# A twelve-layer network on one core: the first weights of most layers beside the ring, and a convolution's first block in two passes

## The chip, the cores and the metric

The kernel runs on one core of a Trainium2 chip. The metric is the device time of one execution in microseconds, the median of three. TensorE multiplies, VectorE and ScalarE do elementwise work and read PSUM, GpSimd does small roots and issues loads of vectors and tables, and the SyncE queue (SP) issues the loads of the weights.

## What is computed

The reference sends 256 tokens of 1024 channels in float32 through twelve layers, a mixer and a feed-forward network in turn:

```
LAYERS = ("rwkv", "ffn", "moba", "ffn", "conv", "ffn", "near", "ffn", "hyena", "ffn", "conv", "ffn")
first block (layers 0 to 3):   x = layer_norm(ALPHA * x + mixer(x));  x = layer_norm(ALPHA * x + swiglu_ffn(x))
second block (layers 4 to 11): x = x + mixer(rmsnorm(x));             x = x + swiglu(rmsnorm(x))
conv mixer:                    (b_gate * depthwise_conv3(c_gate * u)) @ w_out, with b_gate, c_gate, u = split(h @ w_in)
```

The mixers are a recurrent time mix with a decay (rwkv), two kinds of attention (moba, near), a gated convolution of width 3 (conv) and one by a Fourier transform (hyena). Each has an input projection of 1024 to 3072 channels and an output projection of 1024 to 1024; a feed-forward network goes to 2 x 2816 and back.

## The kernel before

**Weights in quarters.** All large weights come as 588 quarters of 128 x 1024 float32 (512 KB), in the order of their use: 24 + 8 for a mixer, 44 + 22 for an ffn. For each, SP loads `raw` (L333, L339), ScalarE writes a rounded copy `w_hi` (L1169), VectorE writes the rest `w_lo = raw - w_hi` (L1554), and TensorE multiplies in three passes, hi by hi, hi by lo and lo by hi, in the fp32r format. `raw`, `w_hi` and `w_lo` are rings of four slots; quarter q stands in slot q % 4. SP loads a slot anew when its `w_lo` is done (a loop with a wait on `w_lo[s]`); `split` waits for the load and for `w_used`, TensorE's sign that it has used what stood in the slot. `ahead(q, n)` splits the quarters q + 4 and on.

**Blocks.** An input projection goes in blocks of four quarters. `block_tokens` has the tokens as stationary operand, 128 at a time, and moves 512 columns of weights (L361). `block_channels`, for conv and hyena, has 128 columns of weights as stationary operand and moves all 256 tokens (L419). `project` is the output projection (L448), tokens 0 to 127 (t = 0) first in its last four rows, so that the next layer's norm can start on them. `half_done` tells VectorE of each finished half row.

**Boundaries.** `residual` of VectorE adds the projection to the residual X (`add`, L1604 and L1606), forms the moments (layer norm: `add_with_stats`, `moments`, `centred` L1621, `normed` L1628) or waits for the squares of ScalarE (`square`, L1203) and the root of GpSimd (L2374), and writes the normed tokens (`rms_normed`, L1636). TensorE turns them to channels (`turn`, L468), ScalarE takes their rounded copy (`operand`, L1181) and VectorE the rest (`operand`, L1575, which signals `operand_ready`). Among these steps stand the splits of the next layer's first four quarters, whose slots come free only as the last rows of the projection are used. TensorE does t = 0 of the first block, turns t = 1, then does t = 1 (`first_block`); before a conv or hyena layer it waits for both halves and then does all 256 tokens. Matmuls on the identity without use (`keep_busy`, L383) stand in the gaps.

```
            for t in range(TT):
                for i in range(4):
                    if i % 2 == 0:
                        pe.wait_ge(m["operand_ready"], due(m["operand_ready"]))
                    if t == 0:
                        if src is X:
                            keep_busy((0, 0, 3, 1)[i])
                        pe.wait_ge(w_lo[(q + i) % SLOTS], nth(q + i))
                    mm = part_tokens(q, i, 0, t)
```

**Order.** Every engine works its own program in order; semaphores tie them together. The order was written out by hand.

## Time and profile before

| | us |
|---|---|
| median of 3 runs | 2048.99 (2047.09 to 2050.7) |
| the profiled execution, its own time | 2047.56 |
| its span in the profile | 2045.8 |
| TensorE busy | 1986.2 |
| VectorE busy | 1276.6 |
| ScalarE busy | 908.8 |
| GpSimd busy | 161.6 |

Times in the profile are in microseconds from the start of the span, unless marked ns. Busy time counts the `keep_busy` matmuls too. Matmuls are pipelined: the time from the start of one to the start of the next is what one costs, and is shorter than its own duration. The mean granted clock of TensorE is 0.995 of 2.4 GHz.

### The profile page before, as it was taken

What the parts mean: (1) busy time and instruction counts of PE and PEld (TensorE: products, weight loads), DVE (VectorE), ACT (ScalarE), POOL (GpSimd) and SP (SyncE); (2) the same over time, 40 slices, a digit from 0 to 9 for tenths busy, and PEclk for the clock granted to TensorE, in tenths of its full rate; (3) what the DMA queues carried; (4) which work ended last, traced back from release to release, by engine and by line L of the source; (5) the groups of instructions that cost most, each with busy time, mean ns of one, the idle gap of its engine ahead of it and who ended that gap; (6) DMA issues with size and microseconds to landing.
All of it is one profiled execution on the core that took longest, in us unless ns stands there. A gap on an engine that the chain in (4) does not pass through costs nothing.

```text
span 2045.8 us, 32584 instructions
## 1 busy us (share of the span) xinstructions
PE 1986.2 (97%) x12754; PEld 1615.7 (79%) x12754; DVE 1276.6 (62%) x1623; ACT 908.8 (44%) x1282; POOL 161.6 (8%) x198
## 2 busy tenths in 40 slices
PE   7999999999999999999999999999999999999999
PEld 6689688878678879888878678877766888897887
DVE  7774755477665556655667655577886554575554
ACT  4452354434444434444555454434434444434442
POOL 2252100000010010000003011001100000000000
PEclk9999999999999999999999999999999999999999
DMA  8321265555166554565455257553323555555554
GB/s 302 114 63 45 98 216 182 189 170 180 62 201 200 196 185 165 171 210 184 166 190 191 73 167 226 200 185 124 104 83 126 192 185 187 174 167 187 183 171 155
DMA packets 93040, 335.95 MB, mean 164 GB/s; under 512 B 11230, under 2 KB 11364, under 8 KB 92623
## 3 DMA queue, kind: packets, MB, share of 16 engines
q1 hardware_dynamic: 85824, 311.62, 45.9%
q0 software_dynamic: 7120, 22.95, 3.8%
q8 instruction: 72, 1.18, 0.2%
q14 instruction: 24, 0.20, 0.0%
HBM read 332.43 MB, written 1.05 MB: 163 GB/s over the span
## 4 chain that ended last, share of the span: by engine, by line
PE 87%; DVE 8%; issue 2%; POOL 2%; ACT 2%; DMA 0%; SPq 0%; DVEq 0%; ACTq 0%; POOLq 0%
PE acc L361 42%; PE acc L448 20%; PE acc L419 9%; DVE w_lo L1554 2%; PE acc L920 2%; PE aux L841 1%; PE aux L468 1%; PE aux L625 1%; PE aux L876 1%; POOL rstd L2371 1%; PE aux L908 1%; DVE operand_lo L1575 1%; PE aux L897 1%; ACT w_hi L1169 1%; POOL rstd L2374 1%
## 5 line engine op out<-in xcount | busy, mean ns | idle before, releaser
L1554 DVE TENSOR_TENSOR w_lo<-w_raw,w_hi 128x1024 fp32r<-128x1024 f32 x588 | 716.7, 1224 | 569.5 <-ACT w_hi L1169 562.5
L1169 ACT ACTIVATE w_hi<-w_raw 128x1024 fp32r<-128x1024 f32 x588 | 620.6, 1059 | 786.6 <-PE acc L361 456.4
L361 PE MATMUL acc<-w_hi,operand_hi 128*128 128x512 f32 x1344 | 536.7, 399 | 27.0 <-DVE operand_lo L1720 12.1
L361 PE MATMUL acc<-w_hi,operand_lo 128*128 128x512 f32 x1344 | 526.8, 392 | 0.0
L361 PE MATMUL acc<-w_lo,operand_hi 128*128 128x512 f32 x1344 | 526.3, 392 | 0.0
L361 PEld LDWEIGHTS acc<-w_hi,operand_hi 128*128 128x128 f32 x1344 | 253.6, 189 | 91.8 <-DVE operand_lo L1575 15.4
L361 PEld LDWEIGHTS acc<-w_hi,operand_lo 128*128 128x128 f32 x1344 | 253.5, 189 | 54.0
L361 PEld LDWEIGHTS acc<-w_lo,operand_hi 128*128 128x128 f32 x1344 | 254.0, 189 | 50.3 <-issue 0.5
L448 PE MATMUL acc<-w_hi,hidden_hi 128*128 128x512 f32 x528 | 207.9, 394 | 0.0
L448 PE MATMUL acc<-w_hi,hidden_lo 128*128 128x512 f32 x528 | 205.9, 390 | 0.0
L448 PE MATMUL acc<-w_lo,hidden_hi 128*128 128x512 f32 x528 | 205.6, 389 | 0.0
L419 PE MATMUL acc<-operand_hi,w_hi 128*128 128x256 f32 x576 | 171.1, 297 | 0.8 <-DVE operand_lo L1575 0.8
L419 PE MATMUL acc<-operand_hi,w_lo 128*128 128x256 f32 x576 | 164.0, 285 | 0.0
L419 PE MATMUL acc<-operand_lo,w_hi 128*128 128x256 f32 x576 | 164.0, 285 | 0.0
L419 PEld LDWEIGHTS acc<-operand_hi,w_hi 128*128 128x128 f32 x576 | 111.6, 194 | 9.3 <-issue 8.0
L448 PEld LDWEIGHTS acc<-w_hi,hidden_hi 128*128 128x128 f32 x528 | 99.1, 188 | 24.5 <-issue 3.7
L448 PEld LDWEIGHTS acc<-w_hi,hidden_lo 128*128 128x128 f32 x528 | 99.1, 188 | 21.1
L448 PEld LDWEIGHTS acc<-w_lo,hidden_hi 128*128 128x128 f32 x528 | 99.3, 188 | 19.8
L419 PEld LDWEIGHTS acc<-operand_hi,w_lo 128*128 128x128 f32 x576 | 111.5, 194 | 3.6 <-issue 3.6
L419 PEld LDWEIGHTS acc<-operand_lo,w_hi 128*128 128x128 f32 x576 | 111.4, 193 | 0.0
L1181 ACT ACTIVATE operand_hi<-aux 128x512 fp32r<-128x512 f32 x52 | 28.9, 596 | 86.2 <-PE aux L468 85.7
L2383 POOL TENSOR_SCALAR stat<-stat 128x1 f32<-128x1 f32 x16 | 4.8, 303 | 741.1 <-ACT token_scratch L1203 741.0
(474 smaller groups left out, 2111.7 us busy)
## 6 DMA issues: line engine op xcount, KB each, us to landing
w_raw<-in_weights SPq DMA_DIRECT2D x588, 512.0 KB, 3.4
ln_gain<-in_gains POOLq DMA_DIRECT2D x7, 512.0 KB, 5.0
bias_at<-in_rpb POOLq DMA_DIRECT2D x12, 256.0 KB, 5.1
ln_gain<-in_ln_g POOLq DMA_DIRECT2D x4, 512.0 KB, 3.9
ln_bias<-in_ln_b POOLq DMA_DIRECT2D x4, 512.0 KB, 5.1
vec_rw<-in_vec POOLq DMA_DIRECT2D x3, 512.0 KB, 5.6
l_rw<-in_lora SPq DMA_DIRECT2D x1, 1152.0 KB, 10.6
iclr_rw<-in_xT SPq DMA_DIRECT2D x2, 512.0 KB, 4.6
```

The costliest lines, as they stand in the source:

```text
L361: mm = pe.matmul(acc[:, 2 * pair + t, :], (ah, al)[x][:, kt, t * P:(t + 1) * P], W[w][:, s, kk * 512:(kk + 1) * 512], start=(kt == 0 and ( ...
L419: mm = pe.matmul(acc[:, 2 * pair + c // 2, (c % 2) * SEQ:(c % 2 + 1) * SEQ], W[w][:, s, kk * 512 + c * P:kk * 512 + (c + 1) * P], (ah, al) ...
L448: mm = pe.matmul(acc[:, 2 * t + c, :], (hi, lo)[x][:, kt, t * P:(t + 1) * P], W[w][:, s, c * 512:(c + 1) * 512], start=(kt == 0 and (x, w) ...
L468: mm = pe.transpose(aux[:, 2 * t + kt // 4, (kt % 4) * P:(kt % 4 + 1) * P], src[:, t, kt * P:(kt + 1) * P], back(ident[:, P - 1:P]) if bac ...
L625: mm = pe.matmul(ps(4 + u % 2)[half_of(1 - s), kt * CH:(kt + 1) * CH], NM[of, u // 2, u % 2, kt, :], INVT[of, u // 2, u % 2, kt, :], start ...
L841: mm = pe.transpose(aux[:, odd, kk * SEQ + t * P:kk * SEQ + (t + 1) * P], HM[:, odd, t, kk * P:(kk + 1) * P], ident[:])
L876: mm = pe.matmul(aux[:, h, t * SEQ:t * SEQ + keys], QT[of, p, t * P:(t + 1) * P], KTT2[of, p, 0:keys], start=True, stop=False, skip_group_ ...
L897: mm = pe.transpose(aux[:, 2 + h, k * SEQ + t * P:k * SEQ + (t + 1) * P], PR[:, p % 2, t, h, k * P:(k + 1) * P], ident[:])
L920: mm = pe.matmul(acc[:, 2 * t + c, :], (ah, al)[x][:, kt, t * P:(t + 1) * P], W[w][:, s, c * 512:(c + 1) * 512], start=(kt == 0 and (x, w) ...
L1169: act.activation(whi[:, s, :], raw[:, s, :], ACT.Copy).then_inc(w_hi[s], 1)
L1181: act.activation(ah[:, 4 * h:4 * h + 4, t * P:(t + 1) * P], aux[:, 2 * t + h, :].rearrange("p (k n) -> p k n", n=P), ACT.Copy)\
L1554: dve.tensor_tensor(wlo[:, s, :], raw[:, s, :], whi[:, s, :].bitcast(F32), ALU.subtract).then_inc(w_lo[s], 1)
```

## The change

The first four quarters of the nine layers 1, 2, 3, 4, 5, 7, 9, 10 and 11 leave the ring and get four slots of their own (`SPARE_HI`, and `SPARE_LO`, which shares its storage with `SPARE_RAW`). SP's loop is written out; it issues each spare load behind a stated ring quarter of the layer before (`spare_beside`), the first of four after a wait for `spare_used`, and after rwkv, near and hyena for one more semaphore. ScalarE and VectorE split them at stated places of the layer before; a split waits until all four are loaded. From the boundaries of these layers the splits go, and VectorE's steps stand in another order. `first_block` issues no `keep_busy` among its first quarters where they are spare; the conv layers' first block becomes `first_channels`, two passes of 128 tokens, and the turn of t = 0 moves into the projection before layer 10. Near and hyena still take their first quarters from the ring. Four semaphores for constants become one, to make room. The waits on `w_used`, `w_lo` and `w_hi` go by functions (`used_of`, `lo_of`, `hi_of`) that pick the ring's or the spare semaphore.

```diff
-        n = q // SLOTS + 1
+        n = in_ring[q] // SLOTS + 1
...
+    def of(sems, spare, q, at=None):
+        return (m[spare], beside_ring[q] + 1) if q in beside_ring else (sems[slot(q)], nth(q, at))
...
+    def weight(x, q):
+        return (SPARE_HI, SPARE_LO)[x][:, beside_ring[q] % SLOTS, :] if q in beside_ring else W[x][:, slot(q), :]
...
+    spared = [n for n, kind in enumerate(layers) if n and kind not in ("near", "hyena")]
+    beside_ring = {start[n] + i: SLOTS * k + i for k, n in enumerate(spared) for i in range(SLOTS)}
+    in_ring = {q: r for r, q in enumerate(q for q in range(quarters) if q not in beside_ring)}
...
-        for q in range(SLOTS):
-            sp.dma_start(raw[:, q, :], A["weights"][q]).then_inc(w_full[q], 16)
-        sp.dma_start(L1[:], A["lora1"]).then_inc(m["rwkv_in"], 16)
-        rest = (quarters - SLOTS) // SLOTS
-        with sp.Fori(0, rest) as i:
-            for s in range(SLOTS):
-                sp.wait_ge(w_lo[s], i + 1)
-                sp.dma_start(raw[:, s, :], A["weights"][bass.ds(i * SLOTS + (SLOTS + s), 1)].rearrange("q p n -> (q p) n"))\
-                  .then_inc(w_full[s], 16)
-        for q in range((rest + 1) * SLOTS, quarters):
-            sp.wait_ge(w_lo[q % SLOTS], nth(q) - 1)
-            sp.dma_start(raw[:, q % SLOTS, :], A["weights"][q]).then_inc(w_full[q % SLOTS], 16)
+        def load_spare(n, i):
+            if i == 0:
+                sp.wait_ge(m["spare_used"], SLOTS * spared.index(n))
+                if layers[n - 1] == "rwkv":
+                    sp.wait_ge(m["y_ready"], TT)
+                elif layers[n - 1] == "near":
+                    sp.wait_ge(m["scores_ready"], PAIRS * sum(kind in ("moba", "near") for kind in layers[:n]))
+                elif layers[n - 1] == "hyena":
+                    sp.wait_ge(m["operand_ready"], operands(n - 2) + 4)
+            sp.dma_start(raw_of(start[n] + i), A["weights"][start[n] + i]).then_inc(m["spare_full"], 16)
+        def spare_beside(n, k):
+            at = {"ffn": (FB * 4, FB * 4 + 4, FB * 4 + 8, FB * 4 + 12), "conv": (4, 10, 16, 22), "moba": (IN_Q, IN_Q + 1, IN_Q + 2, IN_Q + 3)}
+            at = at.get(layers[n - 1], (IN_Q + OUT_Q - 1,) * SLOTS)
+            for i in range(SLOTS):
+                if at[i] == k:
+                    load_spare(n, i)
+        for n in range(len(layers)):
+            for k in range((start[n + 1] if n + 1 < len(layers) else quarters) - start[n]):
+                q = start[n] + k
+                if q not in beside_ring:
+                    if in_ring[q] >= SLOTS:
+                        sp.wait_ge(w_lo[slot(q)], nth(q) - 1)
+                    sp.dma_start(raw_of(q), A["weights"][q]).then_inc(w_full[slot(q)], 16)
+                if n == 0 and k == SLOTS - 1:
+                    sp.dma_start(L1[:], A["lora1"]).then_inc(m["rwkv_in"], 16)
+                if n + 1 in spared:
+                    spare_beside(n + 1, k)
...
-                        if src is X:
+                        if src is X and q not in beside_ring:
                             keep_busy((0, 0, 3, 1)[i])
-                        pe.wait_ge(w_lo[(q + i) % SLOTS], nth(q + i))
+                        pe.wait_ge(*lo_of(q + i))
...
+        def first_channels(q):
+            for t in range(TT):
+                for i in range(4):
+                    if i % 2 == 0:
+                        pe.wait_ge(m["operand_ready"], due(m["operand_ready"]))
+                    if t == 0:
+                        pe.wait_ge(*lo_of(q + i))
+                    for kk in range(2):
+                        kt = 2 * i + kk
+                        for c in range(4):
+                            for x, w in PE_PASSES:
+                                at = (c % 2) * SEQ + t * P
+                                mm = pe.matmul(acc[:, c // 2, at:at + P], weight(w, q + i)[:, kk * 512 + c * P:kk * 512 + (c + 1) * P],
+                                               (ah, al)[x][:, kt, t * P:(t + 1) * P], start=(t == 0 and kt == 0 and c % 2 == 0 and (x, w) == (0, 0)),
+                                               stop=(t == TT - 1 and kt == KT - 1 and c % 2 == 1 and (x, w) == (1, 0)), skip_group_check=True)
+                    if t == TT - 1:
+                        mm.then_inc(used_of(q + i)[0], 1)
+                    elif i == 2:
+                        turn(tok, 1, halves=True)
...
-            project(q + FB * 4, FK, HH, HL, between, first=1, near_end={"moba": X, "near": tok}.get(following))
+            project(q + FB * 4, FK, HH, HL, between, first=1, near_end={"moba": X, "near": tok, "conv": tok if normed else None}.get(following))
...
         def conv(q, first):
             if first:
-                keep_busy(7)
-            turn(tok, 0, halves=True)
-            keep_busy(2 if first else 3)
-            turn(tok, 1, halves=True)
-            keep_busy(2 if first else 1, bank=0)
-            for j in range(6):
+                keep_busy(4)
+                turn(tok, 0, halves=True)
+                keep_busy(1)
+            first_channels(q)
+            for j in range(1, 6):
                 if j >= 2:
                     freed = m["c_done"] if j < 4 else m["z_done"]
                     pe.wait_ge(freed, due(freed))
-                block_channels(q + 4 * j, j % 2, operand_waits=(j == 0))
+                block_channels(q + 4 * j, j % 2)
...
+            if q in beside_ring:
+                act.wait_ge(m["spare_full"], 16 * SLOTS * (beside_ring[q] // SLOTS + 1))
+            else:
+                s = slot(q)
+                act.wait_ge(w_full[s], 16 * nth(q) if at is None else at[0] * (16 * at[1] // SLOTS) + 16 * nth(q))
+                if in_ring[q] >= SLOTS:
+                    act.wait_ge(w_used[s], nth(q) - 1 if at is None else at[0] * (at[1] // SLOTS) + nth(q) - 1)
+            act.activation(weight(0, q), raw_of(q), ACT.Copy).then_inc(hi_of(q)[0], 1)
...
-            if channels and n < LAYER_NORMS:
-                ahead(q - 4, 1)
+            if early:
+                if rms:
+                    square(0)
+                if layers[n] == "near":
+                    split(q + 2)
+                operand(0)
+                if layers[n] == "near":
+                    split(q + 3)
+                if rms:
+                    square(1)
+                operand(1)
+                return
             if rms:
                 square(0)
...
+                    if k in SPARE_ROWS:
+                        spare(q + FFN_Q, SPARE_ROWS.index(k), 1)
...
+                if near and p == PAIRS - 1:
+                    spare(q + IN_Q + OUT_Q, 0, 2)
+                elif not near and p >= SLOTS:
+                    spare(q + IN_Q + OUT_Q, p - SLOTS, 1)
...
+            spare(q + IN_Q + OUT_Q, 0, 4)
             ahead(q + IN_Q, OUT_Q - 4)
...
+                normed(0)
+                add_with_stats(1, 0)
                 if rms:
-                    ahead(q - 4, 1)
-                normed(0)
-                if not rms:
-                    ahead(q - 4, 1)
-                    operand(0, (0,))
-                    ahead(q - 3, 1)
-                    operand(0, (1,))
-                add_with_stats(1, 0)
+                    rms_normed(0)
+                operand(0)
                 add_with_stats(1, 1)
                 moments(1)
-                if not rms:
-                    ahead(q - 2, 1)
                 centred(1)
-                if not rms:
-                    ahead(q - 1, 1)
                 normed(1)
                 if rms:
-                    rms_normed(0)
                     rms_normed(1)
-                    both_operands()
-                    ahead(q - 3, 3)
-                else:
-                    operand(1)
+                operand(1)
...
+            if layers[n] == "near":
+                split(q + 2)
             rms_normed(0)
+            if early:
+                operand(0, (0,))
+                add(1, 0)
+                operand(0, (1,))
+                add(1, 1)
+                if layers[n] == "near":
+                    split(q + 3)
+                rms_normed(1)
+                operand(1)
+                return
...
+            spare(q + IN_Q + OUT_Q, 0, 2)
             ahead(q + IN_Q, OUT_Q - 4)
+            spare(q + IN_Q + OUT_Q, 2, 2)
...
-                pool.wait_ge(w_used[(q + 3 * k // 2) % SLOTS], nth(q + 3 * k // 2))
+                pool.wait_ge(*used_of(q + max(SLOTS - 1, 3 * k // 2)))
...
-            if n < LAYER_NORMS:
-                for t in range(TT):
+            for t in range(TT):
+                if n < LAYER_NORMS:
                     layer_root(t)
-            if rms:
-                for t in range(TT):
+                if rms:
                     rms_root(t)
```

`SPARE_ROWS = (6, 9, 12, 15)`. The calls of `spare` in VectorE's program stand at the same places as those of ScalarE.

## Rows read from the trace of the kernel before

**Rows 1.** The page: its span and TensorE's busy time.

```profile
span 2045.8 us, 32584 instructions
...
PE 1986.2 (97%) x12754; PEld 1615.7 (79%) x12754; DVE 1276.6 (62%) x1623; ACT 908.8 (44%) x1282; POOL 161.6 (8%) x198
```

**Rows 2.** Waits of TensorE: total us, times, longest us.

```profile
PE acc L361 <- DVE operand_lo L1575: 11.3, 9, 1.8
```

**Rows 3.** The critical chain, merged: start us, us, what.

```profile
268.10 10.93 PE acc L361 x48
...
483.35 1.75 PE aux L866 x16
...
773.42 69.13 PE acc L419 x576
...
1424.20 1.73 PE aux L1007 x16
```

**Rows 4.** Timeline, TensorE's weight loads, start of layer 10: start us, us, what.

```profile
1760.16 0.19 PEld L419 LDWEIGHTS acc<-operand_hi,w_hi 128*128 128x128 f32 x1 [1.11 <-DVE operand_lo L1575]
...
1760.27 0.19 PEld L419 LDWEIGHTS acc<-operand_hi,w_lo 128*128 128x128 f32 x1
```

**Rows 5.** Timeline of the boundary from layer 0 to 1.

```profile
235.09 1.41 DVE L1628 SCALAR_TENSOR_TENSOR residual<-residual,rstd,ln_bias 128x512 f32<-128x512 f32 x2 [0.53 <-POOL rstd L2374]
...
237.55 0.68 DVE L1575 TENSOR_TENSOR operand_lo<-aux,operand_hi 128x512 fp32r<-128x512 f32 x1
...
243.77 1.22 DVE L1554 TENSOR_TENSOR w_lo<-w_raw,w_hi 128x1024 fp32r<-128x1024 f32 x1
...
243.93 1.46 POOL L2374 TENSOR_TENSOR rstd<-stat,minus_half 128x1 f32<-128x1 f32 x1 [8.96 <-DVE stat L1616]
...
247.36 1.41 DVE L1628 SCALAR_TENSOR_TENSOR residual<-residual,rstd,ln_bias 128x512 f32<-128x512 f32 x2
...
249.01 1.03 PE L468 MATMUL aux<-ident_sb,residual 128*128 128x128 f32 x8
...
251.02 0.50 PE L361 MATMUL acc<-w_hi,operand_hi 128*128 128x512 f32 x1 [0.97 <-DVE operand_lo L1575]
```

**Rows 6.** Timeline of VectorE, end of layer 2 and boundary to 3.

```profile
540.93 1.23 DVE L1554 TENSOR_TENSOR w_lo<-w_raw,w_hi 128x1024 fp32r<-128x1024 f32 x1 [0.35 <-ACT w_hi L1169]
542.07 1.01 DVE L2033 TENSOR_REDUCE nmax_at<-aux 128x2 f32<-128x256 f32 x2
...
564.24 1.41 DVE L1628 SCALAR_TENSOR_TENSOR residual<-residual,rstd,ln_bias 128x512 f32<-128x512 f32 x2 [0.54 <-POOL rstd L2374]
...
579.44 1.29 DVE L1575 TENSOR_TENSOR operand_lo<-aux,operand_hi 128x512 fp32r<-128x512 f32 x2 [1.52 <-ACT operand_hi L1181]
```

**Rows 7.** Timelines of TensorE and VectorE, boundary from layer 3 to 4.

```profile
759.75 6.17 PE L383 MATMUL aux<-ident_sb 128*128 128x512 f32 x14
...
769.18 1.41 DVE L1636 SCALAR_TENSOR_TENSOR token_scratch<-residual,rstd,first_rms_gain 128x512 f32<-128x512 f32 x2 [0.79 <-POOL rstd L2374]
...
772.85 0.68 PE L419 MATMUL acc<-operand_hi,w_hi 128*128 128x256 f32 x1
```

**Rows 8.** The critical chain, end of layer 4 and start of 5.

```profile
848.48 15.30 PE acc L448 x66
867.87 6.19 PE acc L361 x18
874.93 17.70 PE acc L361 x78
```

**Rows 9.** Windows of that boundary: busy by engine, clock, DMA share, GB/s.

```profile
868.00:872.00 4.00, 4.00 (x12) 2.84 (x13) 4.00 (x6) 2.62 (x4) 0.88 (x2) 0.66 0.70 231
872.00:876.00 4.00, 4.00 (x22) 3.35 (x21) 2.67 (x5) 1.09 (x2) 0.00 (x0) 0.91 0.76 229
```

**Rows 10.** The tile w_raw from 1755 to 1775 us, its seven loads.

```profile
DMA to landing us min/median/max: 3.7/5.6/7.0
```

**Rows 11.** Timeline of VectorE, boundary from layer 9 to 10.

```profile
1751.30 1.41 DVE L1636 SCALAR_TENSOR_TENSOR token_scratch<-residual,rstd,ln_gain 128x512 f32<-128x512 f32 x2 [1.87 <-POOL rstd L2374]
```

**Rows 12.** Timeline of VectorE, boundary 6 to 7, and hyena's projection.

```profile
1192.01 1.41 DVE L1636 SCALAR_TENSOR_TENSOR token_scratch<-residual,rstd,ln_gain 128x512 f32<-128x512 f32 x2 [1.86 <-POOL rstd L2374]
...
1541.42 2.48 DVE L1575 TENSOR_TENSOR operand_lo<-aux,operand_hi 128x512 fp32r<-128x512 f32 x4 [0.78 <-ACT operand_hi L1181]
1550.46 5.31 DVE L1554 TENSOR_TENSOR w_lo<-w_raw,w_hi 128x1024 fp32r<-128x1024 f32 x4 [6.55 <-ACT w_hi L1169]
```

More of the change, by code:

```diff
@@ L311, in nth, with operands, slot, hi_of @@
     def nth(q, at=None):
-        n = q // SLOTS + 1
+        n = in_ring[q] // SLOTS + 1
         return n if at is None else at[0] * (at[1] // SLOTS) + n
+    def operands(n):
+        return sum({"rwkv": 8, "hyena": 8, "moba": 4 + PAIRS, "near": 4 + PAIRS}.get(kind, 4) for kind in layers[:n + 1])
+    def slot(q):
+        return in_ring[q] % SLOTS
+    def of(sems, spare, q, at=None):
+        return (m[spare], beside_ring[q] + 1) if q in beside_ring else (sems[slot(q)], nth(q, at))
+    def hi_of(q, at=None):
+        return of(w_hi, "spare_hi", q, at)
+    def lo_of(q, at=None):
+        return of(w_lo, "spare_lo", q, at)
+    def used_of(q, at=None):
+        return of(w_used, "spare_used", q, at)
+    def weight(x, q):
+        return (SPARE_HI, SPARE_LO)[x][:, beside_ring[q] % SLOTS, :] if q in beside_ring else W[x][:, slot(q), :]
+    def raw_of(q):
+        return SPARE_RAW[:, beside_ring[q] % SLOTS, :] if q in beside_ring else raw[:, slot(q), :]
     start = {}
@@ L1175, in ahead, with spare @@
                     split(q + k + SLOTS, at)
+        def spare(q, first, n):
+            for k in range(first, first + n):
+                if q in beside_ring:
+                    split(q + k)
         def operand(t):
@@ L1559, in ahead, with spare @@
                     split(q + k + SLOTS, at)
+        def spare(q, first, n):
+            for k in range(first, first + n):
+                if q in beside_ring:
+                    split(q + k)
         def used(q, at=None):
-            dve.wait_ge(w_used[q % SLOTS], nth(q, at))
+            dve.wait_ge(*used_of(q, at))
         def step(instruction):
@@ L1961, in ffn @@
                         hyena_tables(k)
+                    if k in SPARE_ROWS:
+                        spare(q + FFN_Q, SPARE_ROWS.index(k), 1)
                 return
@@ L2080, in attention @@
                     split(q + IN_Q + p - 2 + SLOTS)
+                if near and p == PAIRS - 1:
+                    spare(q + IN_Q + OUT_Q, 0, 2)
+                elif not near and p >= SLOTS:
+                    spare(q + IN_Q + OUT_Q, p - SLOTS, 1)
         def conv(q, layer):
```

108 lines of the change are left out of this document (55 added, 53 removed).

## The prediction

> **What bounds the kernel now.** I read the page, then TensorE's waits, the critical chain, and the timeline around each layer boundary. TensorE is busy nearly all of the 2045.8 us span [rows 1]; its largest repeated wait is for `operand_lo`, the split of the next layer's input, at the boundaries [rows 2]. Inside a layer nothing waits: a 512-column matmul comes every 0.2277 us (10.93/48), a 256-column one every 0.120 us (69.13/576) [rows 3]. Time is lost only between layers, and there busy shares mislead: the boundary is filled with `keep_busy` matmuls that compute nothing. At layer 3 to 4 it is L383, 14 in 6.17 us, 0.43 apart [rows 7].
>
> **What the boundaries cost today, and who is late.** At layer 0 to 1 VectorE does normed(0), split, operand half, split, operand half, then the second 128 tokens with two more splits among them. Normed(0) starts at 235.09, the splits of that stretch take 1.22 each, normed(1) starts at 247.36 [rows 5]; the turn starts at 249.01 and its second pass at 251.02, 2.0 us later [rows 5]. So for the second pass VectorE is late, not a transfer. Conv to ffn loses 2.0 us before its first matmul (865.9 to 867.87 [rows 8]) and, in the next 8 us, runs partly at the lower of the two clock levels (granted 0.66, then 0.91 of 2.4 GHz): 4 x 0.34 + 4 x 0.09 = 1.7 us [rows 9].
>
> **Gains, boundary by boundary.** I replayed VectorE's queue in the new order with the old durations: scalar ops on 512 columns 0.7 us (two 1.41), a full-width pass 1.3 (an estimate from two such), the layer norm's root 1.46 on GpSimd [rows 5].
> - 0 to 1 and 1 to 2 (layer norms). The four splits go, and so do the waits for `w_lo` and the 4 `keep_busy`. But operand(0) now stands behind add_with_stats(1, 0), which waits for `half_done`; first operand half 239.3 instead of 237.55, so the first pass starts 1.6 later. Its 24 matmuls (5.5 us) end at 245.5; normed(1) starts at 244.2 instead of 247.36, so the turn starts at 245.5 instead of 249.01, and the second pass at 247.5 instead of 251.02: 3.5 us gained. At 0 to 1 the last two spare splits stand in front of add(0, 0) and cost 0.6 of it: 2.9. In layer 1 the splits at k = 6, 9, 12, 15 fit VectorE's free 1.5 us a quarter; without this cover each would cost up to 1.2.
> - 2 to 3: same replay from normed(0) at 564.24, second pass 575.2 instead of about 580.2 (the operands' lower half starts at 579.44 [rows 6]): 5.0. Against it, in the attention's pair loop the spare splits for p = 4 and 5 come on top of the ring's (540.93 to 542.07, and the maximum follows with no gap [rows 6]): 1.1 us of TensorE each; at p = 6 and 7 VectorE has room. Net 2.5 with 0.3 for a later add.
> - 4 to 5 and 10 to 11 (conv to ffn). The first half operand no longer waits behind a split and an add: the first pass starts when the project ends, 865.9 instead of 867.87, without the clock loss. rms_normed(1) follows its root at 869.4, not 871.29. Second pass 872.6 instead of 876.3 (six matmuls after 874.93 [rows 8]): 3.7. Four spare splits (4.6 us) ahead of the project's four ring splits make the first of those 0.4 late: 3.3 each.
> - 6 to 7 (near to ffn): two spare splits stand in front of add(0, 0), one in front of rms_normed(0), which starts 2.7 after its 1192.01 [rows 12]. The waits saved later do not make this good: 1.1 lost.
> - 8 to 9 (hyena to ffn): the SP queue waits for the operands (done 1543.9 [rows 12]) before the four spare loads, and ScalarE's spare split waits for all four. Four loads land in about 7.0 [rows 10], 1551.3. Behind stand the ring splits, whose first `w_lo` started at 1550.46 [rows 12]; it is now done at 1555.8, and TensorE needs it at 1553.1 (16 steps of 0.68 after 1542.2). 2.7 lost there, 0.8 by spare splits in front of the adds, 2.9 won at the boundary itself: 0.6 lost.
> Sum: 2.9 + 3.5 + 2.5 + 3.3 + 3.3 - 1.1 - 0.6 = 13.8 us gained.
>
> **The convolutions' first block.** It had 96 matmuls of 256 columns at 0.120, 11.5 us; it gets 192 of 128 columns. The trace has no such matmul with w_hi. Bounds from rows: half of the 256-column pace, 0.060, below; the 256-column pace, 0.120, as an ordinary top; and 0.215 as the worst, twice the column rate of the plain f32 `keep_busy` (0.43 for 512 columns). I take 0.110. The weights of each matmul must be loaded, and two successive loads of this kind at a block's start are 0.11 apart [rows 4]; plain f32 with only 64 moving columns still comes every 0.108 (1.73/16), the 128-column transposes every 0.109 [rows 3]. So a short matmul is bound by its weight load. The Trainium skill ("TensorE: Matmul & The Clock Gate", section Back-to-back issue gap) gives about 0.081 us sustained for a moving operand of 128 columns in a stream of load and matmul pairs; by it the total would come out 9 us lower than mine. The trace does not show that pace for any such pair with a full 128 x 128 load: its nearest ones are the 0.108 and 0.109 above.
> - 9 to 10: the turn goes into the project, the first pass starts at 1754.9 instead of 1760.16 [rows 4]. rms_normed(0) at 1751.30 [rows 11] allows it. 72 matmuls, turn 0.9, 24, 96: end 1754.9 + 0.9 + 192 x 0.110 = 1776.9; before 1760.2 + 11.5 = 1771.7. 5.1 lost.
> - 3 to 4: VectorE's chain for the second tokens gets rms_normed(0) (with its wait for the root) and operand(0) put in: rms_normed(1) starts at 773.0 instead of 769.18 [rows 7], turned at 774.9, then 24 + 96 matmuls: 788.1; before 773.4 (its second matmul; the first is held from 772.85 [rows 7]) + 11.5 = 784.9. 3.2 lost.
>
> **The SP queue in a convolution.** This is the term that I hold most damaging. load_spare(5, 0) is issued behind ring quarter k = 4 of layer 4, and first waits for `spare_used` 16, which includes the four quarters of this very layer's first block. SP runs ahead of TensorE, so it stands there until that block is over; queued behind it are the loads of k = 5, 6 and 7. When the block ends (F), SP issues the spare load and k = 5. A load of a burst lands 3.7 to 7.0 us after issue, median 5.6 [rows 10]; I take 5.0, as the burst is not yet at its fullest. Then 1.06 + 1.22 for the two splits and 0.5 for issue and signals: `w_lo` at F + 7.8. TensorE finishes k = 4 at F + 2.9. Stall 4.9 us; from the bounds 3.6 to 6.9. Twice, layers 4 and 10: 9.8 us. The CT copy queued behind these splits on ScalarE is needed a block later, at no cost. After such an idle stretch the clock can fall, as it did after the 2.0 us before the stretch in [rows 9] at a cost of 1.7 to 1.9; it did not after every such idle, so I count it once: 1.9.
>
> **Sum.** +13.8 - 3.2 - 5.1 - 9.8 - 1.9 = -6.2 us. The profiled execution's own time is 2047.56 (span 2045.8, 1.8 around it); the changed one would be 2053.8. The median of the runs is 2048.99, 1.4 above it; I predict 2055 us. Within 0.2% (4.1 us) is about what a measurement here cannot tell from no change, so 6 is just past it.
>
> **Rivals.**
> - Short matmuls are not bound by the weight load (0.060 to 0.085 each). End of first block falls by (96 + 24) per unit at 3 to 4 and 192 at 9 to 10, 312 in all: at 0.070, 12.5 us less, 2042.5; at 0.085, 2047. It decides the sign below 0.090. (The back-to-back figure of the Trainium skill, above, belongs to this rival.) For it: loads overlap the running matmul in all long streams, where 0.120 equals load as well as matmul. Against: 0.108 for 64 columns [rows 3]. Chance 0.14.
> - The SP wait costs nothing, because loads of k = 5 to 7 are issued or land earlier than I read. Then 9.8 + 1.9 come back: 2043, faster. Against: the order in the SP program is strict, and the count includes the block. Chance 0.12.
> - Short matmuls cost 0.2 and more: 312 x 0.1 = 31 us more, 2086 and above. No row shows it. Chance 0.08.
> - The boundaries give more or the conv stalls less than worked out, by some 4 us together, and it ends between 2046 and 2052: chance 0.18. For it: my replay charges every queue in order and gives no slack back.
> - My forecast, 2051 to 2062: 0.48.
>
> Faster by over 0.2% (below 2045): both first rivals, 0.26. Within: 0.21. Slower: 0.53. The range takes in both signs, 2041 to 2063; that of the likeliest alone is 2051 to 2062.
>
> **What the changed profile would show.** Matmuls of the first block with 128x128 moving, 0.110 apart (0.06 or 0.2 refutes). In layers 4 and 10 one TensorE idle of about 5 us after k = 4, released through `w_lo` by a load landing, and none before. SP's wait before the spare load ending at the block's end. No L383 in ffn and moba first blocks; second pass at layer 0 to 1 some 2.0 us after its turn, total of that boundary 3 shorter. In hyena's project one wait of about 3 us. If the two conv stretches are not 8 us or more longer each, the prediction is wrong.

## The result, and the profile after

The changed kernel takes 2062.68 us (median of 5 runs, 2060.28 to 2063.21), the kernel before 2048.99 (median of 5, 2044.25 to 2050.70): ratio 1.0071, 95% interval 1.0058 to 1.0083. It is slower, by about 14 us where 6 were forecast: 0.7 us above the range that was called likeliest (2051 to 2062), inside the wide one (2041 to 2063). The profiled execution took 2062.68, its span is 2060.9 against 2045.8 [rows 1], so 15.1 us have to be found. Of the versions further down, G has one execution of eleven in a slower state (2215.6 us at a granted clock of 0.85), which its ratio leaves out.

The page after, span and TensorE's busy time:

```profile
span 2060.9 us, 31241 instructions
...
PE 1993.0 (97%) x12902; PEld 1634.5 (79%) x12902; DVE 1274.5 (62%) x1623; ACT 904.7 (44%) x1282; POOL 160.8 (8%) x198
```

TensorE is "busy" 6.8 us longer, although it multiplies the same numbers: in the blocks of short matmuls it works at a worse rate, and at a lower clock every matmul lasts longer. A busy share doesn't show either.

The waits after (total us, times, longest us):

```profile
PE acc L476 <- DVE w_lo L1660: 8.4, 2, 4.2
PE acc L419 <- DVE operand_lo L1687: 8.4, 7, 1.8
...
SPq L382 <- PE acc L498: 83.8, 2, 44.3
```

The wait of [rows 2] fell from 11.3 to 8.4 us, as meant. A new one, two times 4.2 us, stands in `block_channels` (L476), which never waited for weights before. The third row is its cause: SP stands before a spare load (L382) twice, up to 44.3 us, until the first block (L498) is over.

The critical chain after, merged, in layers 4, 8 and 10 (start us, us, what):

```profile
757.87 8.26 PE acc L498 x72
767.25 13.36 PE acc L498 x120
781.01 4.36 DMA w_raw<-in_weights
787.76 57.52 PE acc L476 x456
...
1548.09 6.86 DMA w_spare_raw<-in_weights
1556.06 2.36 DVE w_spare_lo L1660 x2
1559.61 12.33 PE acc L527 x42
...
1784.06 4.28 DMA w_raw<-in_weights
1790.73 56.26 PE acc L476 x456
```

The short matmul costs 13.36/120 = 0.1113 us. Transfers of weights are on the chain three times. And 456 matmuls of 256 columns take 57.52 and 56.26 us, where the pace of [rows 3] makes 456 x 0.12 = 54.7: behind each stall 2.8 and 1.5 us more are lost. The same in layer 8: 42 matmuls, 12.33 for 9.6.

The stall of layer 4 in the timeline (start us, us, engine, line, what, count, idle before and its releaser), SP, ScalarE, VectorE and TensorE in turn:

```profile
780.63 0.33 SPq L382 DMA_DIRECT2D w_spare_raw<-in_weights  x1
...
785.39 1.06 ACT L1250 ACTIVATE w_hi<-w_raw 128x1024 fp32r<-128x1024 f32 x1 [16.56 <-DMA w_raw<-in_weights]
...
786.48 1.23 DVE L1660 TENSOR_TENSOR w_lo<-w_raw,w_hi 128x1024 fp32r<-128x1024 f32 x1 [16.39 <-ACT w_hi L1250]
...
783.24 0.28 PE L476 MATMUL acc<-operand_lo,w_hi 128*128 128x256 f32 x1
787.76 0.58 PE L476 MATMUL acc<-operand_hi,w_hi 128*128 128x256 f32 x1 [4.24 <-DVE w_lo L1660]
```

First block ends, SP is let go at 780.63, quarter k = 5 is issued behind the spare load, lands 4.4 us later, is split twice, and TensorE goes on at 787.76. Idle of 16 us on the two splitting engines shows how long nothing had come. Windows of the same place (length, busy of each engine, granted clock, DMA share, GB/s):

```profile
784.00:788.00 4.00, 0.24 (x1) 0.24 (x2) 1.23 (x1) 1.30 (x2) 0.00 (x0) 0.84 0.93 353
788.00:792.00 4.00, 4.00 (x20) 4.00 (x21) 2.49 (x3) 3.72 (x4) 0.00 (x0) 0.50 0.80 297
792.00:796.00 4.00, 4.00 (x29) 4.00 (x29) 2.42 (x2) 1.06 (x1) 0.00 (x0) 0.81 0.90 274
```

The granted clock is 0.50 of 2.4 GHz behind the stall, the lower level, and 20 matmuls pass in 4 us instead of 33.

The boundary from layer 0 to 1, which answers to the last row of [rows 5]:

```profile
247.98 0.51 PE L419 MATMUL acc<-w_spare_hi,operand_hi 128*128 128x512 f32 x1 [0.97 <-DVE operand_lo L1687]
```

The second pass starts at 247.98 for 251.02.

**Where the time went, layer by layer.** VectorE's first add to the residual is a mark that every layer has, in every version. For layers 3 and 4 the two rows after are

```profile
745.23 0.69 DVE L1717 SCALAR_TENSOR_TENSOR residual<-residual,acc 128x512 f32<-128x512 f32 x1 [1.16 <-PE acc L527]
...
861.37 0.69 DVE L1719 TENSOR_TENSOR residual<-residual,acc 128x512 f32<-128x512 f32 x1 [1.13 <-PE acc L527]
```

and before they are

```profile
752.55 0.69 DVE L1604 SCALAR_TENSOR_TENSOR residual<-residual,acc 128x512 f32<-128x512 f32 x1 [1.16 <-PE acc L448]
...
857.76 0.69 DVE L1606 TENSOR_TENSOR residual<-residual,acc 128x512 f32<-128x512 f32 x1 [1.12 <-PE acc L448]
```

116.14 us for 105.21, so the interval of layer 4 (the boundary 3 to 4 and the layer) grew by 10.9. All intervals, as the difference from the kernel before in its profiled execution, us:

| version | 0 | 1 | 2 | 3 | 4 | 5 | 6 | 7 | 8 | 9 | 10 | 11 |
|---|---|---|---|---|---|---|---|---|---|---|---|---|
| changed kernel | +0.7 | -3.6 | +0.1 | -4.5 | +10.9 | -3.4 | +1.9 | +0.6 | +6.3 | -2.6 | +11.9 | -3.2 |
| A spare loads later | -0.5 | -3.6 | +2.8 | -4.6 | +3.9 | -3.3 | +1.9 | +0.6 | +4.9 | -3.7 | +6.2 | -3.2 |
| B one pass | +0.9 | -3.6 | +0.1 | -4.5 | +12.0 | -3.4 | +1.9 | +0.5 | +5.7 | -2.7 | +10.9 | -3.2 |
| C ring first | +1.4 | -3.6 | +1.5 | -4.6 | +9.5 | -3.4 | +1.3 | -0.3 | +4.9 | -4.3 | +13.1 | -3.2 |
| D ten idle matmuls | +4.4 | -3.6 | +1.6 | -4.6 | +12.5 | -3.4 | +1.3 | +0.5 | +5.3 | -2.6 | +14.8 | -3.2 |
| E five idle matmuls | +1.2 | -3.6 | +0.1 | -4.6 | +8.3 | -3.4 | +1.8 | +0.6 | +6.9 | -2.8 | +10.6 | -3.2 |
| F A, one pass, cover | +3.5 | -3.6 | -1.4 | -4.5 | +8.8 | -3.4 | +1.8 | +0.6 | +6.5 | -2.8 | +1.7 | -3.2 |
| G A, 7 and 9 from the ring | +2.0 | -3.6 | +1.3 | -4.5 | +3.9 | -3.4 | 0.0 | 0.0 | -0.2 | 0.0 | +6.2 | -3.2 |
| H spare 1, 2, 3, 5, 11 | +0.8 | -3.6 | +0.1 | -4.6 | +0.9 | -3.4 | -0.5 | 0.0 | +2.0 | +0.6 | +0.9 | -3.3 |
| I H, splits moved | +0.4 | -3.7 | -3.0 | -4.5 | 0.0 | -3.4 | -0.4 | 0.0 | +0.4 | 0.0 | 0.0 | -3.2 |
| J H, 4 and 10 spare, old order | +2.1 | -3.6 | 0.0 | -4.6 | +0.1 | -3.3 | -0.4 | 0.0 | 0.0 | 0.0 | +0.6 | -3.2 |
| K idle matmuls in hyena | +1.3 | -3.6 | +0.2 | -4.5 | +10.9 | -3.4 | +2.0 | +0.7 | +6.5 | -3.7 | +12.1 | -3.3 |

Where two versions have the same code, layers 1, 3, 5 and 11 agree to 0.1 us. The others don't. In layer 2 (-1.4 to +2.8) and layer 8 the granted clock falls at other places from one execution to the next; in layer 6 it falls at the boundary from 5 in some (+1.8 to +2.0) and not in C and D (+1.3). In layer 0 (-0.5 to +4.4) the clock stays at 0.97 or more in windows of 4 us in the kernel before, the changed one, A, C, D, G and J, so D's +4.4 isn't the clock's (F's +3.5 may be in part, 0.69 from 196 to 200), and no run here says what it comes from. The stalled layers 4 and 10 differ by 1.4 and 1.2 in C. Hyena differs most: layers 8 and 9 together are at +3.7, +1.2, +3.0, +2.7, +4.1 and +3.7 in the changed kernel, A, B, D, E and F, whose code there is the same. TensorE's one wait in hyena's output projection, 3.49 us in the changed kernel, is 1.53 in A, 2.35 in B, 3.50 in D, 4.80 in E and 3.05 in F. Nothing as small as these spreads is read from the table below without another row.

### The profile page after: what moved, and what is told of

Read it like the earlier page. It is cut to its first block, busy times and chain, and to the rows that moved or that the text cites. A ratio compares the mean times of both kernels' runs of the same rounds, so it can differ in the third digit from the quotient of the medians.

```text
span 2060.9 us, 31241 instructions
## 1 busy us (share of the span) xinstructions
PE 1993.0 (97%) x12902; PEld 1634.5 (79%) x12902; DVE 1274.5 (62%) x1623; ACT 904.7 (44%) x1282; POOL 160.8 (8%) x198
## 4 chain that ended last, share of the span: by engine, by line
PE 87%; DVE 8%; ACT 2%; issue 1%; POOL 1%; DMA 1%; SPq 0%; DVEq 0%; ACTq 0%; POOLq 0%
PE acc L419 42%; PE acc L527 19%; PE acc L476 8%; DVE w_lo L1660 2%; PE acc L498 2%; PE acc L999 2%; PE aux L920 1%; PE aux L547 1%; DVE w_spare_lo L1660 1%; PE aux L704 1%; POOL rstd L2495 1%; PE aux L987 1%; ACT w_hi L1250 1%; PE aux L955 1%; PE acc L691 1%
## 5 line engine op out<-in xcount | busy, mean ns | idle before, releaser
L1660 DVE TENSOR_TENSOR w_lo<-w_raw,w_hi 128x1024 fp32r<-128x1024 f32 x552 | 670.4, 1224 | 545.7 <-ACT w_hi L1250 541.8
L1250 ACT ACTIVATE w_hi<-w_raw 128x1024 fp32r<-128x1024 f32 x552 | 580.7, 1059 | 740.8 <-PE acc L419 448.1
L419 PE MATMUL acc<-w_hi,operand_hi 128*128 128x512 f32 x1232 | 489.3, 397 | 14.1 <-DVE operand_lo L1833 12.2
L419 PE MATMUL acc<-w_hi,operand_lo 128*128 128x512 f32 x1232 | 482.5, 392 | 0.0
L419 PE MATMUL acc<-w_lo,operand_hi 128*128 128x512 f32 x1232 | 481.9, 391 | 0.0
L419 PEld LDWEIGHTS acc<-w_hi,operand_hi 128*128 128x128 f32 x1232 | 232.3, 189 | 62.4 <-DVE operand_lo L1833 12.0
L419 PEld LDWEIGHTS acc<-w_hi,operand_lo 128*128 128x128 f32 x1232 | 232.1, 188 | 49.0
L419 PEld LDWEIGHTS acc<-w_lo,operand_hi 128*128 128x128 f32 x1232 | 232.4, 189 | 46.8 <-issue 0.5
L476 PE MATMUL acc<-operand_hi,w_hi 128*128 128x256 f32 x512 | 154.7, 302 | 8.9 <-DVE w_lo L1660 8.4
L476 PE MATMUL acc<-operand_hi,w_lo 128*128 128x256 f32 x512 | 147.6, 288 | 0.0
L476 PE MATMUL acc<-operand_lo,w_hi 128*128 128x256 f32 x512 | 147.6, 288 | 0.0
L476 PEld LDWEIGHTS acc<-operand_hi,w_hi 128*128 128x128 f32 x512 | 101.3, 198 | 16.8 <-DVE w_lo L1660 8.8
L476 PEld LDWEIGHTS acc<-operand_hi,w_lo 128*128 128x128 f32 x512 | 101.2, 198 | 3.3 <-issue 3.3
L476 PEld LDWEIGHTS acc<-operand_lo,w_hi 128*128 128x128 f32 x512 | 100.9, 197 | 0.0
```

The lines of the kernel that those rows point to most:

```text
L419: mm = pe.matmul(acc[:, 2 * pair + t, :], (ah, al)[x][:, kt, t * P:(t + 1) * P], weight(w, q + i)[:, kk * 512:(kk + 1) * 512], start=(kt = ...
L476: mm = pe.matmul(acc[:, 2 * pair + c // 2, (c % 2) * SEQ:(c % 2 + 1) * SEQ], weight(w, q + i)[:, kk * 512 + c * P:kk * 512 + (c + 1) * P], ...
L1250: act.activation(weight(0, q), raw_of(q), ACT.Copy).then_inc(hi_of(q)[0], 1)
L1660: dve.tensor_tensor(weight(1, q), raw_of(q), weight(0, q).bitcast(F32), ALU.subtract).then_inc(lo_of(q)[0], 1)
```

## The experiments

**A. Spare loads of the conv layers later** (x_sp_later).

```diff
-"conv": (4, 10, 16, 22)
+"conv": (8, 12, 16, 20)
```

> The changed kernel with one edit: beside a conv layer the four spare loads stand behind ring quarters 8, 12, 16 and 20 instead of 4, 10, 16 and 22, so that quarters 4 to 7 are issued before SP waits for spare_used. Theory (SP's wait holds back the loads of quarters 5 to 7; TensorE then idles 4.24 us in layer 4 and 4.16 us in layer 10, and the clock falls after each idle stretch, 2.8 and 1.5 us): both idle stretches and both falls of the clock go, the profiled span falls by 4.24 + 4.16 + 2.8 + 1.5 = 12.7 us, from 2060.9 to about 2048, within 0.2% of the kernel before. Rival (the later splits of the spare quarters, on ScalarE and VectorE at the end of the conv layer, come too late for the next boundary): the two stalls go, but 3 to 8 us come back at the boundaries 4 to 5 and 10 to 11.

Measured: 2047.97 us, ratio to the kernel before 1.0000 (0.9990 to 1.0009). Layers 4 and 10 lost 7.0 and 5.7 us, 12.7 together, to the tenth what was expected; layers 5 and 11 kept their gains (-3.3, -3.2), so the rival falls. (The span fell by 13.8; the other 1.1 is the balance of layers 0, 2, 8 and 9, whose code is unchanged.) Timeline of SP in this version, and its wait:

```profile
771.53 0.33 SPq L398 DMA_DIRECT2D w_raw<-in_weights  x1
782.05 0.33 SPq L382 DMA_DIRECT2D w_spare_raw<-in_weights  x1
...
SPq L382 <- PE acc L498: 20.3, 2, 10.2
```

SP still waits for the end of the block (782.05), but it comes to that wait later, after four more ring loads, so the longest is 10.2 us and not 44.3; and the last load that the next block needs at once has gone out at 771.53. What stood behind the wait in the queue did the harm: with nothing urgent there, a wait that ends at the same event costs TensorE nothing.

**B. The first block of the conv layers in one pass** (x_one_pass).

```diff
-            first_channels(q)
+            turn(tok, 1, halves=True)
+            block_channels(q, 0, operand_waits=True)
```

> The changed kernel with the conv layers' first block in one pass of 256 tokens again (96 matmuls of 256 columns for 192 of 128), its weights still from the spare slots. Theory (the short matmul costs 0.111 us, bound by its weight load, the long one 0.120: the two passes cost 21.3 us a block against 11.5, and give back only the wait for the second half's tokens): 3 to 4 comes out about even or a little better (0 to 3 us less), 9 to 10 better by 3 to 5.5 us; the span falls by 3 to 8 us. Rival (the overlap of the first pass with the second half's norm is worth its price once the weights are there early): the span stays or rises.

Measured: 2062.42 us, 1.0066 (1.0052 to 1.0080), layer 4 +12.0, layer 10 +10.9: no difference in sum. The rival's side, but the edit had also taken away what covered the gap. TensorE now idles 8.18 us ahead of the turn in layer 4, and the windows from 760 to 772 us have a granted clock of 0.50. Its timeline in this version:

```profile
766.05 1.97 PE L547 MATMUL aux<-ident_sb,token_scratch 128*128 128x128 f32 x8 [8.18 <-DVE token_scratch L1750]
```

The mean clock of the execution is 0.985 for 0.991. Not told apart; F does it for layer 10.

**C. Hyena: the ring's splits ahead of the spare ones** (x_ring_first), for ScalarE and VectorE alike.

```diff
-            spare(q + IN_Q + OUT_Q, 0, 2)
             ahead(q + IN_Q, OUT_Q - 4)
-            spare(q + IN_Q + OUT_Q, 2, 2)
+            spare(q + IN_Q + OUT_Q, 0, 4)
```

> The changed kernel with one edit in the hyena layer: ScalarE and VectorE split the ring's quarters of its output projection first and all four spare quarters behind them. Theory (the two spare splits that stand ahead wait for a load that SP issued late and hold up the ring's splits behind them: TensorE idles 3.49 us, and the clock then falls, 3.4 us): the idle stretch and the fall go, the span falls by 5 to 7 us. Rival (the ring's splits are late by their own loads): the idle stretch keeps more than 2 us, the span moves by under 2 us.

Measured: 2058.91 us, 1.0051 (1.0038 to 1.0064). VectorE's timeline after, and in this version:

```profile
1556.06 2.36 DVE L1660 TENSOR_TENSOR w_spare_lo<-w_spare_raw,w_spare_hi 128x1024 fp32r<-128x1024 f32 x2 [9.38 <-ACT w_spare_hi L1250]
1558.34 4.63 DVE L1660 TENSOR_TENSOR w_lo<-w_raw,w_hi 128x1024 fp32r<-128x1024 f32 x4
```

```profile
1553.90 5.31 DVE L1659 TENSOR_TENSOR w_lo<-w_raw,w_hi 128x1024 fp32r<-128x1024 f32 x4 [7.62 <-ACT w_hi L1250]
1559.13 4.62 DVE L1659 TENSOR_TENSOR w_spare_lo<-w_spare_raw,w_spare_hi 128x1024 fp32r<-128x1024 f32 x4
...
1563.67 1.28 DVE L1718 TENSOR_TENSOR residual<-residual,acc 128x512 f32<-128x512 f32 x2
```

The ring's quarters had lain ready while VectorE waited 9.38 us for the spare ones. Now TensorE has no idle stretch there and its clock is 1.00, as expected. Layers 8 and 9 together went from +3.7 to +0.6, 3.1 us and not 5 to 7: the spare splits are now in front of the first add, which waits for VectorE and not for TensorE, and the fall of the clock had been counted too high (K). The 3.1 itself is no firm price, as the same code stands between +1.2 and +4.1 in the table; that the idle stretch is gone is what this version shows.

**D and E. Matmuls without use in the stall** (x_fill, y_fill5), in the block with j = 1, ten and five of them.

```diff
+                if fill and i == 1:
+                    keep_busy(10)
                 pe.wait_ge(*lo_of(q + i))
```

> The changed kernel with ten matmuls on the identity, without use, ahead of the wait for the second quarter of the second block in both conv layers (10 x 0.43 = 4.3 us, the length of the idle stretch). Everything else stays, the stall too. Theory (the clock falls because TensorE idled there): the stall keeps its 4.2 us each, the granted clock stays at 1.0 behind it, the span falls by 2.8 + 1.5 = 4.3 us, give or take 1. Rival (the clock falls for another reason, or the fall costs nothing): no change, within 1 us.

Measured: 2067.67 us, 1.0088 (1.0074 to 1.0102), slower, the opposite of what was expected. The reason was the cost: a `keep_busy` matmul is two records of 0.43, ten took 8.2 us, 4 more than the stall. So again with five:

> The changed kernel with five matmuls on the identity ahead of the wait for the second quarter of the second block in both conv layers. The ten of the run before took 8.16 us there and not 4.3 (each of them is two records of 0.43), so they overran the stall by 4 us; five take 4.2, the length of the stall. Theory (the clock falls because TensorE idled): granted clock 1.0 from 784 to 800, the interval from the first add of layer 3 to that of layer 4 shrinks from 10.9 us above the kernel before to 8, that of layer 10 from 11.9 to 10.4. Rival (the fall has another cause, or costs nothing): both intervals stay as they were.

Measured: 2059.59 us, 1.0053 (1.0040 to 1.0066). Its windows:

```profile
784.00:788.00 4.00, 4.00 (x11) 1.55 (x9) 1.15 (x1) 1.59 (x2) 0.00 (x0) 1.00 1.02 404
788.00:792.00 4.00, 4.00 (x33) 3.88 (x33) 2.82 (x4) 3.78 (x5) 0.00 (x0) 1.00 0.85 281
792.00:796.00 4.00, 4.00 (x35) 4.00 (x35) 2.06 (x2) 1.29 (x2) 0.00 (x0) 1.00 1.00 339
```

The clock is 1.00 throughout, 33 matmuls where 20 had been, the stall itself is as long as before. Layer 4 went from +10.9 to +8.3, layer 10 from +11.9 to +10.6: 2.6 and 1.3, for 2.8 and 1.5 expected. The rival falls: here the idle stretch makes the clock fall, and that fall has its own price beside the stall.

**F. A, and one pass with the cover of the kernel before** (y_one_pass): as B, but 7, 2 and 2 matmuls without use ahead of and behind the turns of layer 4, and 3 and 1 in layer 10.

> The changed kernel with the spare loads of the conv layers behind quarters 8, 12, 16 and 20 (as in the run that removed the stalls) and the first block in one pass of 256 tokens, now with as many matmuls without use in the gaps as the kernel before has (11 and 4), since with 5 and 0 the clock fell over that block (mean granted clock of the execution 0.985 for 0.991). Against that run (layer 4 3.9 us over the kernel before, layer 10 6.2 over): theory (two passes cost more than they give back): layer 4 comes to 0 to 2, layer 10 to 0 to 2, span 5 to 8 us shorter, about 2041. Rival (the two ways are even, as the run with one pass and few such matmuls came out): both within 1 us of 3.9 and 6.2.

Measured: 2050.92 us, 1.0007 (0.9998 to 1.0015). Layer 10 went from +6.2 to +1.7: two passes cost 4.5 us there, and the theory holds for this layer. Layer 4 went from +3.9 to +8.8, against both. VectorE's timeline at that boundary in this version:

```profile
755.36 1.42 DVE L1751 SCALAR_TENSOR_TENSOR token_scratch<-residual,rstd,first_rms_gain 128x512 f32<-128x512 f32 x2 [0.60 <-POOL rstd L2500]
760.88 1.29 DVE L1689 TENSOR_TENSOR operand_lo<-aux,operand_hi 128x512 fp32r<-128x512 f32 x2 [4.10 <-ACT operand_hi L1270]
...
768.87 1.41 DVE L1751 SCALAR_TENSOR_TENSOR token_scratch<-residual,rstd,first_rms_gain 128x512 f32<-128x512 f32 x2 [1.84 <-POOL rstd L2500]
```

VectorE waits 4.10 us for the operand of the first 128 tokens, and the whole norm of the second 128 stands behind it: they are normed 13.5 us after the first (768.87 - 755.36), before it was 2.2 (769.18 [rows 7] and this one):

```profile
766.98 1.41 DVE L1636 SCALAR_TENSOR_TENSOR token_scratch<-residual,rstd,first_rms_gain 128x512 f32<-128x512 f32 x2 [0.44 <-POOL rstd L2374]
```

This order only pays with two passes, which use the first tokens meanwhile. J agrees from the other side: one pass and early weights, but the old order and cover, and layer 4 is at +0.1 in place of +8.8.

**G. A, and layers 7 and 9 from the ring** (y_no79).

```diff
-    spared = [n for n, kind in enumerate(layers) if n and kind not in ("near", "hyena")]
+    spared = [n for n, kind in enumerate(layers) if n and kind not in ("near", "hyena") and n not in (7, 9)]
```

> The changed kernel with the conv spare loads behind quarters 8, 12, 16 and 20, and the first quarters of layers 7 and 9 from the ring as in the kernel before (so no spare splits in the near and the hyena layer, and the old order at their ends). Theory (spare weights cost more than they give after near and hyena): layers 6 and 7 come to within 0.5 us of the kernel before together (they were 2.5 over), 8 and 9 too (they were 1.2 to 3.7 over), span 3 to 6 us shorter than with them, about 2043. Rival (the loss there is the clock's and has nothing to do with the spare splits): layers 6 and 7 stay 2 us over.

Measured: 2046.11 us, 0.9988 (0.9979 to 0.9997). Layers 6 to 9 are at 0.0, 0.0, -0.2 and 0.0, so nearly all of the loss there was the spare splits', +2.5 at near and +1.2 (A) to +3.7 at hyena. Some 0.6 of near's 2.5 is the clock's: at the boundary 5 to 6, whose code is the same, it falls in A (0.75, then 0.82) and not here.

**H. Spare quarters for layers 1, 2, 3, 5 and 11 alone** (y_best): G, and layers 4 and 10 from the ring with the kernel before's one pass, order and cover.

> Only layers 1, 2, 3, 5 and 11 have spare quarters; layers 4, 7, 9 and 10 take theirs from the ring, and the boundaries and the first block before conv are those of the kernel before. Theory (each boundary is its own sum): the intervals of layers 1, 2 and 3, 5 and 11 keep their gains of 3.6, 2 to 4, 3.4 and 3.2 us, all the others come to within 0.5 of the kernel before, span 12 to 14 us below the kernel before, about 2033. Rival (the gains need the others, or come back as waits for loads): less than 8 us below.

Measured: 2037.47 us, 0.9946 (0.9933 to 0.9959); the profiled execution's span is 10.1 us below the kernel before, 2 to 4 short of the forecast. Layer 2 gained nothing net, layers 4 and 10 lost 0.9 each, and layer 8 shows +2.0 at a place with G's code: the granted clock is 0.50 to 0.63 from 1524 to 1536 us, where G has 0.84 and 0.73 in two windows of 4 us.

**I. H, with the spare splits moved in moba and conv** (z_best2).

```diff
-                elif not near and p >= SLOTS:
-                    spare(q + IN_Q + OUT_Q, p - SLOTS, 1)
+                elif not near and p == PAIRS - 2:
+                    spare(q + IN_Q + OUT_Q, 0, 3)
...
-            spare(q + IN_Q + OUT_Q, 0, 4)
+            spare(q + IN_Q + OUT_Q, 0, 3)
             ahead(q + IN_Q, OUT_Q - 4)
+            spare(q + IN_Q + OUT_Q, 3, 1)
```

The fourth in moba stands ahead of the last pair's operand.

> The fast version (layers 1, 2, 3, 5 and 11 spare), with the spare splits moved in two layers. In moba they stood behind pairs 4 to 7, one each, and pairs 4 and 5 then took 6.9 us for 5.77, since VectorE splits two quarters in a pair; now three stand behind pair 6 and one ahead of the last pair's operand, where VectorE waits 2.50 and 1.99 us. In conv four stood ahead of the ring's splits, and TensorE waited 0.56 and 0.2 us for the ring; now three ahead, one behind. Theory (a split costs time where VectorE or ScalarE paces the layer, and nothing where it waits): the interval of layer 2 shrinks by 2.3 (pairs) + 1.1 (first add) = 3.4 us, layers 4 and 10 by 0.6 each, span 4 to 5 us below that of the fast version (2035.7), about 2031. Rival (another engine paces those pairs): under 1.5 us in all.

Measured: 2032.54 us, 0.9925 (0.9911 to 0.9939), the fastest version. Layer 2 went from +0.1 to -3.0, layers 4 and 10 from +0.9 to 0.0, 4.9 us as forecast (the span fell by 7.5, the rest in layers 0, 8 and 9, whose code is the same). VectorE in a moba pair, in the changed kernel and in this one:

```profile
534.19 1.23 DVE L1660 TENSOR_TENSOR w_lo<-w_raw,w_hi 128x1024 fp32r<-128x1024 f32 x1 [0.36 <-ACT w_hi L1250]
535.34 1.22 DVE L1660 TENSOR_TENSOR w_spare_lo<-w_spare_raw,w_spare_hi 128x1024 fp32r<-128x1024 f32 x1
536.47 1.01 DVE L2150 TENSOR_REDUCE nmax_at<-aux 128x2 f32<-128x256 f32 x2
```

```profile
533.76 1.23 DVE L1669 TENSOR_TENSOR w_lo<-w_raw,w_hi 128x1024 fp32r<-128x1024 f32 x1 [0.35 <-ACT w_hi L1252]
534.90 1.01 DVE L2172 TENSOR_REDUCE nmax_at<-aux 128x2 f32<-128x256 f32 x2
```

The pair's maximum waits for the split in front of it, and the pair takes 6.9 us for 5.77.

**J. Conv from spare quarters, in the kernel before's order** (z_order): H, with 4 and 10 spare, one pass.

> The fast version (spare: 1, 2, 3, 5, 11), but with the conv layers 4 and 10 from spare quarters too, in one pass, with the kernel before's order of steps on VectorE, ScalarE and GpSimd at these two boundaries and its matmuls without use. It tells the weights from the order. Theory (before a conv layer the tokens come last, not the weights; the changed kernel lost there by its order and its two passes): layers 4 and 10 within 1 us of the fast version (0.9 each over the kernel before), no gain. Rival (early weights are worth 2 us or more at these boundaries too, and only the order of the changed kernel spoilt it): both 2 us or more below the fast version.

Measured: 2036.75 us, 0.9950 (0.9935 to 0.9965), within the intervals of H. Layers 4 and 10 are at +0.1 and +0.6, where H, with the same splits at the end of these layers, has +0.9 and +0.9: within the 1 us of the forecast, and the rival's 2 us don't appear. The weights are worth something all the same, 0.8 and 0.3 us: in layer 4 the first block starts 20.2 us after the mark for 20.9 in H, I and the kernel before (J's chain, then H's):

```profile
766.68 69.00 PE acc L476 x576
...
766.11 69.13 PE acc L476 x576
```

(marks at 746.46 and 745.23). No version joins J's early weights with I's places for the splits.

**K. Matmuls without use in hyena's stall** (w_fill_hyena).

```diff
-            project(q + IN_Q, KT, ah, al, operand_steps(), near_end=tok)
+            project(q + IN_Q, KT, ah, al, {**operand_steps(), (4, 0): lambda: keep_busy(4, bank=4)}, near_end=tok)
```

> The changed kernel with four matmuls on the identity (4 x 0.86 = 3.4 us) in hyena's output projection, ahead of the wait in which TensorE idles 3.49 us. The stall stays. Theory (the clock falls behind the stall because TensorE idled): granted clock 1.0 in the 8 us behind it (it was 0.51 and 0.63 in two stretches of 4 us), and the intervals of layers 8 and 9 together, 3.7 us over the kernel before, shrink by 2 to 3.4. Rival (the fall there is one of those that this layer shows now and then, whatever stands in it): the two intervals stay at 3 or more over the kernel before.

Measured: 2061.80 us, 1.0058 (1.0044 to 1.0072). Windows of TensorE (length, busy, clock, DMA share, GB/s), the changed kernel's and then this one's:

```profile
1558.00:1562.00 4.00, 2.39 (x6) 0.51 0.32 112
1562.00:1566.00 4.00, 4.00 (x13) 0.63 0.81 281
```

```profile
1558.00:1562.00 4.00, 2.94 (x9) 1.00 0.00 0
1562.00:1566.00 4.00, 3.83 (x16) 1.00 0.83 277
```

The clock stays up, so here too it had fallen for the idle stretch. Layers 8 and 9 shrank by only 0.9 us, less than the theory's 2 to 3.4, and stand at 2.8, just under the rival's 3. TensorE's timeline in this version:

```profile
1556.73 3.59 PE L441 MATMUL aux<-ident_sb 128*128 128x512 f32 x8
1561.38 0.50 PE L527 MATMUL acc<-w_hi,operand_hi 128*128 128x512 f32 x1 [1.06 <-DVE w_lo L1660]
...
1571.72 1.03 PE L547 MATMUL aux<-ident_sb,token_scratch 128*128 128x128 f32 x8
```

The wait was 1.2 us longer this time (3.59 filled and 1.06 idle for 3.49), and the 42 matmuls behind it took 10.3 us (1561.38 to 1571.72) for 12.33: 2.0 won by the clock. The 3.4 us in the forecast came from the windows, which count idle time at the lower clock as lost too; from the matmuls it is 12.33 - 42 x 0.2277 = 2.8 at most.

## Why the prediction was wrong

It had the sign, and the stalls that it held most damaging are there, for its reason. The time lies in its wide range alone, and it gave 6 us of 15. By its own steps:

- **The clock after an idle stretch, "I count it once: 1.9": this term failed.** It was sized from a boundary of the kernel before, and taken once for three new stalls. It came in three of three: 2.8 and 1.5 us in layers 4 and 10 (E gives 2.6 and 1.3), 2.0 (K) to 2.8 in layer 8. A fall at the boundary 5 to 6, where the clock was 0.60 for 4 us, adds 0.6 (against C and D) to 0.8. That one isn't the change's: TensorE idles there in the kernel before as well, and with the same code the clock fell in A, B, E, F and K and not in C and D. Together up to 7.9, 6.0 more than counted.
- **The boundaries' gains, 13.8.** By the start of the second pass (247.98 for 251.02, less 0.25 by which the two executions already differed) layer 0 to 1 gave 2.8 for 2.9. The 3.5 of 1 to 2 were 2.7; 2.5 of 2 to 3 were 1.8 by the marks of its second pass, the moba pairs' cost included, as it was in the forecast (I gets 3.1 back in layer 2). 4 to 5 and 10 to 11 gave 2.7 each for 3.3, with 0.6 us lost on the ring's late splits in the conv layer where 0.4 was allowed (I removes it). Near cost 1.8 for 1.1, hyena without its clock about 0.8 for 0.6. In sum 0.1 + 0.8 + 0.7 + 1.2 + 0.7 + 0.2 = 3.7 us short. H, where those late splits are all that sets layers 4 and 10 apart from the kernel before, puts them at 0.9 each; then the two boundaries gave 2.5 and 2.3, the conv blocks below cost 0.2 to 0.3 less each, and the total is nearly the same.
- **The conv first block.** The short matmul costs 0.1113 for 0.110, the pace of the two weight loads in [rows 4]; that the load sets it is argued from this agreement, no version varies it. 3 to 4 cost 3.2 as forecast, 9 to 10 5.6 for 5.1; A and F give 4.5 for the two passes in layer 10. The first and third rivals fall.
- **The SP queue.** The mechanism is confirmed (A), its size 4.24 and 4.16 for 4.9 each; the load landed after 4.4 us and not 5.0. 1.4 us less than forecast. The second rival falls.

Sum of the misses: 6.0 + 3.7 + 0.5 - 1.4 = 8.8 of the 8.9 us between the forecast's 6.2 and the span's 15.1. That it closes so well proves little: the parts are cut from the same intervals, and hyena's 0.8 is what was left of them after 2.8 for the clock. With K's 2.0 it is 1.6.

Slips in the prediction's own sums, none of which moves the forecast: the 14 records of L383 are seven matmuls of 0.86 us and not 14 of 0.43; matmuls at 0.2 would add 312 x 0.09 = 28 us to it and not 31; and the first rival, counted as "faster", gives 2047 at 0.085, which is within 0.2%.

## What to carry to other kernels

Whenever a change puts a wait into an in-order queue, look at what stands behind it, not at the wait: A left SP waiting for the same event and won back 12.7 us by sending four loads ahead of the wait. Charge a new idle stretch of TensorE as long as those here (3.5 to 4.2 us) twice, for its length and for the clock behind it, each time and not once; shorter ones went both ways. Early weights paid only where weights or their splits had been late (3.0 to 4.5 us for each of five layers in I); where tokens come last or another engine paces the layer, the same splits cost as much as they gain or more. Taking them away from four of nine layers, with the old order and first block ahead of conv, turned a loss of 0.7% into a gain of 0.5% (H), and better places for the splits made it 0.75% (I).
